# The scan's maxima rows through memory and a GpSimd mask, and the next unit's scores ahead of this unit's updates

## The chip, the cores and the metric

The kernel is one launch on one core of a Trainium2 chip. The metric is device time in microseconds (us), the median over runs; one further execution was profiled.

## The reference

The reference is a two-layer diffusion backbone. Each layer runs four token mixers side by side on 1024 latent tokens and 256 context tokens, projects their outputs, and then applies a feed-forward part (dense in layer 0, top-2 of 8 experts in layer 1). The change concerns the two recurrent mixers, gated linear attention (GLA) and mLSTM, each run forwards and backwards:

```python
def gla_scan(...):      # per chunk
    scores = jnp.where(mask, q_dec @ (k * exp(-cum)).T, 0.0)
    o = scores @ v + q_dec @ s_prev
    s = decay * s + upd
def mlstm_scan(...):    # per chunk
    d_log = jnp.where(mask, cum[..., :, None] - cum[..., None, :] + ig[..., None, :], -jnp.inf)
    m_row = jnp.maximum(inter_log, jnp.max(d_log, axis=-1))
    s = jnp.exp(d_log - m_row[..., None]) * (q @ k.T)
    num = s @ v + w_int * (q @ c_prev)
    out = num / jnp.maximum(jnp.abs(den), jnp.exp(-m_row))
```

## The kernel before, in words

The kernel is a chain of phases. Each phase is a block in which every engine has its own program; the orders are written out by hand and the engines meet at counting semaphores. All engines meet at the end of each block, and GpSimd then clears the phase's semaphores.

Per layer, `phase_side` (L613) computes the gates, the decays, the chunked gating and the Fourier mixing. Its VectorE part fills `mx`, the running maxima of the mLSTM gates: rows 0 to 3 are the four heads forwards, rows 32 to 35 backwards, each 1280 long (L896 to L899). The semaphore `stk` counts three later VectorE steps (L914 to L916).

`phase_scan` (L940) walks U = 20 units per layer, 40 in all: ten tiles of 128 tokens in each of two directions, even units forwards, odd ones backwards. A unit `u` has on each engine:

- TensorE: three transposes into the PSUM banks KT and TR (L987, L989); the maxima rows, spread over all partitions and masked with a large number, into the bank MB (one product of the identity with the mask, L994, then four of a selector with `mx`, L997); the mLSTM scores into SM (L1004); the GLA scores into SG (L1011), which wait for the states of the unit before (`v_st`); the products with the states into OG and OC (L1016, L1018); the GLA output (L1021), after VectorE has masked the scores (`v_sg`); the mLSTM output (L1026); the state updates, GLA's into the upper half of OG (L1031), mLSTM's into SG (L1034).
- ScalarE: a copy of a transpose (L1045), then four exponentials of the maxima rows into `ex` (L1048).
- GpSimd: the queries, masked by head, `qg` (L1066) and `qm` (twice L1068). It may run ahead until the scores of the unit two before are done.
- VectorE: the weighted keys `kw` (L1087), masked copy of the GLA scores `sg` (L1090), the mLSTM weights (L1094), the GLA output added or copied (L1098 or L1100), the mLSTM numerator (`tmp` L1103, `num` L1105), denominator and output (L1108 to L1117), and the state updates `dsg` (L1121), `dsm` (L1123), `Sm` (L1125), `Sg` (L1126), `Sm` again (L1128) and `Sp` (L1130), which ends the unit (`v_st`).

In the first ten units each tile is met for the first time and its output is written; in the last ten it is added to (L1098; L1114 with L1115 in place of L1117). The phase after, `phase_mix_project`, forms the mixers' output and projects it.

Of the kernel before, what the change touches and what calls it, by code (L numbers as in the profile page):

```python
# [18 lines left out]
ACT = mybir.ActivationFunctionType  # L19
# [3 lines left out]
P = 128  # L23
D = 1024
# [588 lines left out]
def phase_side(nc, io, S, l, FM, TM, M, ctx_out):  # L613
# [8 lines left out]
    with Phase(nc, f"side{l}") as ph:  # L622
# [23 lines left out]
        folded, ymm, yev, dused, cdone, zout = (ph.sem(n) for n in (  # L646
            "folded", "y_done", "y_ready", "dft_used", "ctx_z_done", "z_ready"))
# [14 lines left out]
        with nc.Block() as block:  # L662

            @block.sync
            def _(sp):
# [19 lines left out]
                for j in range(NPIECE + (1 if ctx_out else 0)):  # L685
                    piece(j)

# [252 lines left out]
def phase_scan(nc, io, S, l, FM, TM, M):  # L940

    U = 2 * NT
    with Phase(nc, f"scan{l}") as ph:
# [12 lines left out]
        pe_tr, pe_mb, pe_sg, pe_sm, pe_og, pe_om, pe_u = (ph.sem(n) for n in (  # L956
            "transposed", "max_rows_done", "gla_scores_done", "mlstm_scores_done", "gla_out_done", "mlstm_out_done", "updates_done"))
        a_kdt, a_ex = ph.sem("kdt_ready"), ph.sem("ex_ready")
        g_q = ph.sem("masked_q_ready")
# [7 lines left out]
        mx, tg, dcol, qd, kd, em, vx, og, om = (M[k] for k in ("mx", "tg", "dcol", "qd", "kd", "em", "vx", "og", "om"))  # L967
        TR, SG, OG, KT, MB, SM, OI, OC = range(8)
        mq, mk = (2, 3), (4, 5)
        sel8 = c("sel8").rearrange("p (a t) -> p a t", t=P)  # L970
# [6 lines left out]
        with nc.Block() as block:  # L977

            @block.tensor
            def _(pe):  # L980
                for u in range(U):
                    d, n, t = unit(u)

                    if u >= 1:
                        pe.wait_ge(a_kdt, u)
                        pe.wait_ge(v_kw, u)
                    nc.tensor.transpose(ps[:, KT, 0:P], kd[:, d, t], c("ident"))  # L987
                    for j in range(2):
                        x = nc.tensor.transpose(ps[:, TR, (j + 1) * P:(j + 2) * P], FM[:, mk[j], t], c("ident"))  # L989
                    x.then_inc(pe_tr, 1)  # L990

                    if u >= 1:
                        pe.wait_ge(a_ex, u)
                    nc.tensor.matmul(ps[:, MB, :].rearrange("p (h t) -> p h t", t=P), c("ident"),  # L994
                                     c("negF" if d == 0 else "negB").unsqueeze(1).to_broadcast([P, NH, P]), start=True, stop=False, skip_group_check=True)
                    for h in range(NH):
                        x = nc.tensor.matmul(ps[:, MB, h * P:(h + 1) * P], sel8[32 * d:32 * d + 4, 4 * d + h, :], mx[32 * d:32 * d + 4, t],  # L997
                                             start=False, stop=(h == NH - 1), skip_group_check=True)
                    x.then_inc(pe_mb, 1)
# [6 lines left out]
                    x.then_inc(pe_sm, 1)  # L1006
                    if u >= 1:
                        pe.wait_ge(v_st, u)
                    else:
                        pe.wait_ge(v_init, 1)  # L1010
                    nc.tensor.matmul(ps[:, SG, :], kd[:, d, t], qg[:, d, :, :].rearrange("p a b -> p (a b)"),  # L1011
                                     start=True, stop=True).then_inc(pe_sg, 1)
                    if u >= 1:
                        pe.wait_ge(v_og, u)
                        pe.wait_ge(v_om, u)
                    nc.tensor.matmul(ps[:, OG, 0:256], qd[:, d, t], Sp[:, d, :], start=True, stop=False, skip_group_check=True)  # L1016
# [6 lines left out]
                    x.then_inc(pe_og, 1)  # L1023
                    pe.wait_ge(v_w, u + 1)
                    for h in range(NH):
                        x = nc.tensor.matmul(ps[:, OI, h * 65:(h + 1) * 65], ex[:, d, h, :], vx[:, n, h, :], start=True, stop=True)  # L1026
                    x.then_inc(pe_om, 1)

                    pe.wait_ge(a_kdt, u + 1)
                    pe.wait_ge(v_og, u + 1)  # L1030
                    nc.tensor.matmul(ps[:, OG, 256:512], kdt[:, d, :], TM[:, n, 0:256], start=True, stop=True)  # L1031
                    pe.wait_ge(v_kw, u + 1)
                    for j in range(2):
                        x = nc.tensor.matmul(ps[:, SG, j * 130:(j + 1) * 130], kw[:, d, 2 * j:2 * j + 2, :].rearrange("p a b -> p (a b)"),  # L1034
# [1501 lines left out]
```

## Time and profile before

| | us |
|---|---|
| median of 3 runs | 5304.72 |
| lowest, highest | 5299.55, 5308.38 |
| the profiled execution, its own time | 5301.93 |
| its span | 5300.3 |

| engine | busy us | share of the span |
|---|---|---|
| TensorE (PE) | 4911.6 | 93% |
| VectorE (DVE) | 2886.4 | 54% |
| ScalarE (ACT) | 2189.5 | 41% |
| GpSimd (POOL) | 296.0 | 6% |

In the page, PE is the matmul side of TensorE and PEld its weight loads. PEclk is the share of TensorE's full clock that was granted; 1.00 is 2.4 GHz, 0.50 is 1.2 GHz. A matmul of a float32 operand shows as two records, so four matmuls are x8. A row of the timeline can merge several records of one line; its second number is the time from the first record's start to the last one's end, and a square bracket gives how long the engine sat idle before it and what ended that. A row of busy time by stretch gives the stretch, its length, the busy time and count of instructions of PE, PEld, DVE, ACT and POOL in turn, then PEclk, the DMA share and GB/s. Most of the span is the expert phase at the end; the two scans stand at 434 to 613 us and at 2205 to 2383 us.

### The profile page before, as it was taken

How to read it: one execution, taken by the hardware profiler on the slowest of the kernel's cores; microseconds unless marked ns; L12 is line 12 of the kernel's file. 1: busy time of each engine (PE TensorE's matmuls, PEld its weight loads, DVE VectorE, ACT ScalarE, POOL GpSimd, SP SyncE). 2: the span in 40 equal slices, each digit the busy share in tenths (PEclk: the TensorE clock that was granted, in tenths of full speed). 3: DMA queues.
4: the chain of work that ended last, by engine and by line, in shares of the span. 5: the costliest groups of instructions: out<-in, count | busy, mean ns of one | idle time of the engine just before them, and what ended most of it. 6: DMA issues, size and time to landing. Idle time of an engine off the chain costs nothing. (4 is left out here: it accounts for less than half of the span.)

```text
span 5300.3 us, 62249 instructions
## 1 busy us (share of the span) xinstructions
PE 4911.6 (93%) x23448; PEld 4002.3 (76%) x23449; DVE 2886.4 (54%) x2935; ACT 2189.5 (41%) x2253; POOL 296.0 (6%) x303
## 2 busy tenths in 40 slices
PE   6998896999999899897799999999999999999994
PEld 5876665888888678576688888888888888888883
DVE  4367643111133356674764549984696454558476
ACT  3242322111132233313654438773675343446364
POOL 1002210000000010122000000000000000000001
PEclk8998997999999899898899999999999999999996
DMA  5320354222255442104775559995797555569576
GB/s 201 111 85 8 114 189 129 99 96 88 75 191 184 147 141 88 35 1 150 311 286 180 202 192 361 379 354 192 272 378 276 188 200 190 191 231 342 185 285 247
DMA packets 253712, 1003.56 MB, mean 189 GB/s; under 512 B 31840, under 2 KB 96672, under 8 KB 169248
## 3 DMA queue, kind: packets, MB, share of 16 engines
q1 hardware_dynamic: 239152, 945.70, 49.2%
q0 software_dynamic: 10992, 40.90, 2.1%
q10 hardware_dynamic: 3456, 15.47, 0.7%
q8 instruction: 71, 1.16, 0.1%
q14 instruction: 41, 0.34, 0.0%
HBM read 948.77 MB, written 53.22 MB: 189 GB/s over the span
## 5 line engine op out<-in xcount | busy, mean ns | idle before, releaser
L1997 PE MATMUL ps<-moe_gate_up_hi,moe_xh 128*128 128x512 f32 x2464 | 961.8, 390 | 4.4 <-DVE moe_gate_up_lo L2173 4.4
L2173 DVE TENSOR_TENSOR moe_gate_up_lo<-moe_wst,moe_gate_up_hi 128x2048 fp32r<-128x2048 f32 x424 | 952.4, 2285 | 16.6 <-ACT moe_gate_up_hi L2080 16.6
L1997 PE MATMUL ps<-moe_gate_up_hi,moe_xl 128*128 128x512 f32 x2464 | 960.9, 390 | 0.0
L1997 PE MATMUL ps<-moe_gate_up_lo,moe_xh 128*128 128x512 f32 x2464 | 958.9, 389 | 0.0
L2080 ACT CAST moe_gate_up_hi<-moe_wst 128x2048 fp32r<-128x2048 f32 x424 | 791.0, 1920 | 9.7 <-issue 7.0
L2276 DVE TENSOR_TENSOR moe_down_lo<-moe_wst,moe_down_hi 128x2048 fp32r<-128x2048 f32 x210 | 480.2, 2290 | 158.9 <-ACT moe_down_hi L2118 158.2
L2282 DVE TENSOR_TENSOR norm<-moe_sil,ps 128x512 f32<-128x512 f32 x210 | 143.6, 684 | 743.5 <-ACT moe_sil L2124 743.5
L1997 PEld LDWEIGHTS ps<-moe_gate_up_hi,moe_xh 128*128 128x128 f32 x2464 | 462.8, 188 | 101.3 <-DVE moe_gate_up_lo L2173 6.3
L1997 PEld LDWEIGHTS ps<-moe_gate_up_hi,moe_xl 128*128 128x128 f32 x2464 | 462.7, 188 | 96.2
L1997 PEld LDWEIGHTS ps<-moe_gate_up_lo,moe_xh 128*128 128x128 f32 x2464 | 462.8, 188 | 95.4
L2124 ACT ACTIVATE moe_sil<-ps 128x512 f32<-128x512 f32 x210 | 125.9, 600 | 984.2 <-PE ps L1997 984.0
L2118 ACT CAST moe_down_hi<-moe_wst 128x2048 fp32r<-128x2048 f32 x210 | 403.6, 1922 | 72.8 <-PE ps L2017 72.7
L1596 PE MATMUL ps<-hh,up_wh 128*128 128x512 f32 (+1 forms) x1056 | 377.0, 357 | 49.7 <-DVE up_wl L1653 49.7
L2017 PE MATMUL ps<-moe_down_hi,moe_ah 128*128 128x512 f32 x1232 | 399.9, 405 | 9.6 <-DVE moe_al L2287 9.6
L2017 PE MATMUL ps<-moe_down_lo,moe_ah 128*128 128x512 f32 x1232 | 383.3, 392 | 0.0
L2017 PE MATMUL ps<-moe_down_hi,moe_al 128*128 128x512 f32 x1232 | 380.3, 390 | 0.0
L1596 PE MATMUL ps<-hl,up_wh 128*128 128x512 f32 (+1 forms) x1056 | 374.9, 355 | 0.0
L1596 PE MATMUL ps<-hh,up_wl 128*128 128x512 f32 (+1 forms) x1056 | 374.6, 355 | 0.0
L1664 DVE TENSOR_TENSOR up_a<-up_sil,ps 128x512 f32<-128x512 f32 (+1 forms) x66 | 39.6, 600 | 482.0 <-PE ps L1596 481.0
L577 DVE TENSOR_TENSOR proj_w_lo<-proj_w_raw,proj_w_hi 128x1024 fp32r<-128x1024 f32 x122 | 151.6, 1243 | 233.6 <-ACT proj_w_hi L489 232.6
L489 ACT CAST proj_w_hi<-proj_w_raw 128x1024 fp32r<-128x1024 f32 x122 | 127.8, 1047 | 353.8 <-PE ps L433 194.0
L2017 PEld LDWEIGHTS ps<-moe_down_hi,moe_al 128*128 128x128 f32 x1232 | 231.2, 188 | 52.4
(385 smaller groups left out, 7600.1 us busy)
## 6 DMA issues: line engine op xcount, KB each, us to landing
moe_wst<-in_moe_packed SPq DMA_DIRECT2D x634, 1024.0 KB, 6.8
proj_w_raw<-in_w_in_packed SPq DMA_DIRECT2D x122, 512.0 KB, 3.4
down_wst<-in_ffn_w_down SPq DMA_DIRECT2D x66, 512.0 KB, 3.6
up_ada_w<-in_ada_packed SPq DMA_DIRECT2D x12, 2048.0 KB, 8.3
ys_d<-moe_y POOLq DMA_DIRECT2D x15, 1024.0 KB, 4.5
tail_ada_w<-in_ada_packed SPq DMA_DIRECT2D x7, 2048.0 KB, 9.8
a_d<-up_a ACTq DMA_DIRECT2D x22, 640.0 KB, 3.0
FM<-in_w_out_packed SPq DMA_DIRECT2D x27, 512.0 KB, 3.9
```

The source lines that it names most:

```text
L489: nc.scalar.copy(wh[:, p % 2, :], raw[:, p % RAW, :]).then_inc(w_hi, 1)
L577: nc.vector.tensor_tensor(wlo[:, p % 2, :], raw[:, p % RAW, :], wh[:, p % 2, :].bitcast(F32), ALU.subtract).then_inc(split, 1)
L1596: x = nc.tensor.matmul(ps[:, 2 * g + kind, :n], w[:, s, kind, k, :], h[:, k, t0:t0 + n], start=(k == 0 and j == 0), stop=(k == KD - 1 and ...
L1664: nc.vector.tensor_tensor(a[:, s, t0:t0 + n], sil[:, g, :n], ps[:, 2 * g + 1, :n], ALU.mult).then_inc(used, 1)
L1997: x = nc.tensor.matmul(ps[:, 2 * (q % 2) + i, :], xx[:, k, t], w[:, q % 2, k, :], start=(k == 0 and j == 0), stop=(k == KD - 1 and j == 2))
L2017: x = nc.tensor.matmul(ps[:, Y0 + 2 * i + half, :], aa[:, q % 2, i, c, :], w[:, q % 2, c, half * 512:(half + 1) * 512], start=(q == 0 and ...
L2080: nc.scalar.copy(guh[:, q % 2, 4 * j:4 * j + 4, :], wst[:, slot(n), :].rearrange("p (k n) -> p k n", k=4)).then_inc(hi, 1)
L2118: nc.scalar.copy(dnh[:, q % 2, :, :], wst[:, slot(n), :].rearrange("p (k n) -> p k n", k=2)).then_inc(hi, 1)
L2124: nc.scalar.activation(sil[:, :, :], ps[:, 2 * (q % 2):2 * (q % 2) + 2, 0:W], ACT.Silu).then_inc(silu, 1)
L2173: nc.vector.tensor_tensor(gul[:, q % 2, k, :], wst[:, slot(n), :].rearrange("p (k n) -> p k n", k=4), guh[:, q % 2, k, :].bitcast(F32), AL ...
L2276: nc.vector.tensor_tensor(dnl[:, q % 2, :, :], wst[:, slot(n), :].rearrange("p (k n) -> p k n", k=2), dnh[:, q % 2, :, :].bitcast(F32), AL ...
L2282: nc.vector.tensor_tensor(a[:, q % 2, :, :, :].rearrange("p i c f -> p i (c f)"), sil[:, :, :], ps[:, 2 * (q % 2):2 * (q % 2) + 2, W:2 * W ...
```

## The change

- In `phase_side`, SyncE waits for `stk` and stores the eight used rows of `mx` to a new tensor `mx_d` in memory, then waits for both stores.
- In `phase_scan`, SyncE loads for each unit the four rows of its direction and tile, repeated to all 128 partitions, into a ring of four tiles `mxr`. From the fifth unit on it waits for the exponentials of the unit four before.
- GpSimd, after the masked queries of a unit, adds the mask to the loaded tile in place. ScalarE's exponentials read that tile and wait for GpSimd in place of TensorE. The products L994 and L997 are gone.
- TensorE's order is new. For unit `u`: products with the states; GLA output; transposes of `u+1`; mLSTM output of `u`; mLSTM scores and GLA scores of `u+1`; state updates of `u`. The GLA scores wait for VectorE's masked copy of the unit before and no longer for its states.
- The updates of the GLA state go to the upper half of KT, those of mLSTM to the bank that held the maxima, now UM.

```diff
...
+                sp.wait_ge(stk, 1)
+                for d in range(2):
+                    sp.dma_start(S["mx_d"][4 * d:4 * d + 4, :], mx[32 * d:32 * d + 4, :]).then_inc(mxs, 16)
+                sp.wait_ge(mxs, 32)
...
-        g_q = ph.sem("masked_q_ready")
+        g_q, g_mx = ph.sem("masked_q_ready"), ph.sem("max_rows_masked")
+        RING = 4
+        mxr = ph.sb("max_rows", [P, RING, NH, P])
+        mld = [ph.sem(f"max_rows_loaded{s}") for s in range(RING)]
...
-        mx, tg, dcol, qd, kd, em, vx, og, om = (M[k] for k in ("mx", "tg", "dcol", "qd", "kd", "em", "vx", "og", "om"))
-        TR, SG, OG, KT, MB, SM, OI, OC = range(8)
+        tg, dcol, qd, kd, em, vx, og, om = (M[k] for k in ("tg", "dcol", "qd", "kd", "em", "vx", "og", "om"))
+        TR, SG, OG, KT, UM, SM, OI, OC = range(8)
         mq, mk = (2, 3), (4, 5)
-        sel8 = c("sel8").rearrange("p (a t) -> p a t", t=P)
...
-                for u in range(U):
+
+                def turn(u):
                     d, n, t = unit(u)
-
                     if u >= 1:
                         pe.wait_ge(a_kdt, u)
                         pe.wait_ge(v_kw, u)
+                    if u >= 2:
+                        pe.wait_ge(v_st, u - 1)
                     nc.tensor.transpose(ps[:, KT, 0:P], kd[:, d, t], c("ident"))
                     for j in range(2):
-                        x = nc.tensor.transpose(ps[:, TR, (j + 1) * P:(j + 2) * P], FM[:, mk[j], t], c("ident"))
+                        x = nc.tensor.transpose(ps[:, TR, j * P:(j + 1) * P], FM[:, mk[j], t], c("ident"))
                     x.then_inc(pe_tr, 1)
 
-                    if u >= 1:
-                        pe.wait_ge(a_ex, u)
-                    nc.tensor.matmul(ps[:, MB, :].rearrange("p (h t) -> p h t", t=P), c("ident"),
-                                     c("negF" if d == 0 else "negB").unsqueeze(1).to_broadcast([P, NH, P]), start=True, stop=False, skip_group_check=True)
-                    for h in range(NH):
-                        x = nc.tensor.matmul(ps[:, MB, h * P:(h + 1) * P], sel8[32 * d:32 * d + 4, 4 * d + h, :], mx[32 * d:32 * d + 4, t],
-                                             start=False, stop=(h == NH - 1), skip_group_check=True)
-                    x.then_inc(pe_mb, 1)
+                def mlstm_scores(u):
+                    d, n, t = unit(u)
                     if u >= 1:
                         pe.wait_ge(v_w, u)
                     pe.wait_ge(g_q, u + 1)
@@ -1004,15 +1006,27 @@
                         x = nc.tensor.matmul(ps[:, SM, j * 256:(j + 1) * 256], FM[:, mk[j], t],
...
                     x.then_inc(pe_sm, 1)
+
+                def gla_scores(u):
+                    d, n, t = unit(u)
                     if u >= 1:
-                        pe.wait_ge(v_st, u)
-                    else:
-                        pe.wait_ge(v_init, 1)
+                        pe.wait_ge(v_sg, u)
+                    pe.wait_ge(g_q, u + 1)
                     nc.tensor.matmul(ps[:, SG, :], kd[:, d, t], qg[:, d, :, :].rearrange("p a b -> p (a b)"),
                                      start=True, stop=True).then_inc(pe_sg, 1)
+
+                turn(0)
+                mlstm_scores(0)
+                gla_scores(0)
+                for u in range(U):
+                    d, n, t = unit(u)
+                    following = u + 1 < U
+                    pe.wait_ge(v_init, 1)
                     if u >= 1:
                         pe.wait_ge(v_og, u)
                         pe.wait_ge(v_om, u)
+                    if u >= 2:
+                        pe.wait_ge(v_st, u - 1)
                     nc.tensor.matmul(ps[:, OG, 0:256], qd[:, d, t], Sp[:, d, :], start=True, stop=False, skip_group_check=True)
                     for j in range(2):
                         nc.tensor.matmul(ps[:, OC, j * 130:(j + 1) * 130], FM[:, mq[j], t], Sm[:, d, j, :], start=True, stop=True)
...
                     x.then_inc(pe_og, 1)
+                    if following:
+                        turn(u + 1)
                     pe.wait_ge(v_w, u + 1)
                     for h in range(NH):
                         x = nc.tensor.matmul(ps[:, OI, h * 65:(h + 1) * 65], ex[:, d, h, :], vx[:, n, h, :], start=True, stop=True)
                     x.then_inc(pe_om, 1)
-
-                    pe.wait_ge(a_kdt, u + 1)
-                    pe.wait_ge(v_og, u + 1)
-                    nc.tensor.matmul(ps[:, OG, 256:512], kdt[:, d, :], TM[:, n, 0:256], start=True, stop=True)
+                    if following:
+                        mlstm_scores(u + 1)
+                        gla_scores(u + 1)
+
+                    if u >= 1:
+                        pe.wait_ge(v_st, u)
+                    pe.wait_ge(a_kdt, u + 2 if following else u + 1)
+                    nc.tensor.matmul(ps[:, KT, 256:512], kdt[:, d, :], TM[:, n, 0:256], start=True, stop=True)
                     pe.wait_ge(v_kw, u + 1)
                     for j in range(2):
-                        x = nc.tensor.matmul(ps[:, SG, j * 130:(j + 1) * 130], kw[:, d, 2 * j:2 * j + 2, :].rearrange("p a b -> p (a b)"),
+                        x = nc.tensor.matmul(ps[:, UM, j * 130:(j + 1) * 130], kw[:, d, 2 * j:2 * j + 2, :].rearrange("p a b -> p (a b)"),
                                              vx[:, n, 2 * j:2 * j + 2, :].rearrange("p a b -> p (a b)"), start=True, stop=True)
                     x.then_inc(pe_u, 1)
...
                         act.wait_ge(pe_u, u - 1)
                     act.wait_ge(pe_tr, u + 1)
                     nc.scalar.copy(kdt[:, d, :], ps[:, KT, 0:P]).then_inc(a_kdt, 1)
-                    act.wait_ge(pe_mb, u + 1)
+                    act.wait_ge(g_mx, u + 1)
                     for h in range(NH):
-                        x = nc.scalar.activation(ex[:, d, h, :], ps[:, MB, h * P:(h + 1) * P], ACT.Exp,
+                        x = nc.scalar.activation(ex[:, d, h, :], mxr[:, u % RING, h, :], ACT.Exp,
                                                  bias=tg[:, n, 0, d, h:h + 1], scale=-1.0)
                     x.then_inc(a_ex, 1)
 
-            if l == 1:
-                @block.sync
-                def _(sp):
+            @block.sync
+            def _(sp):
+                if l == 1:
                     with nc.allow_non_contiguous_dma(reason="a column set as a vector"):
                         sp.dma_start(cols(S["g2_d"]), S["mod"][:, 1, 40:48, 0]).then_inc(filled, 16)
+                for u in range(U):
+                    d, n, t = unit(u)
+                    if u >= RING:
+                        sp.wait_ge(a_ex, u - RING + 1)
+                    sp.dma_start(mxr[:, u % RING, :, :], S["mx_d"][4 * d:4 * d + 4, t].unsqueeze(0).to_broadcast([P, NH, P])).then_inc(mld[u % RING], 16)
+                if l == 1:
                     sp.wait_ge(filled, 16)
 
...
                         x = nc.gpsimd.tensor_tensor(qm[:, d, 2 * j:2 * j + 2, :], FM[:, mq[j], t].unsqueeze(1).to_broadcast([P, 2, P]),
                                                     bc(c("row2"), P), ALU.mult)
                     x.then_inc(g_q, 1)
+                    pool.wait_ge(mld[u % RING], 16 * (u // RING + 1))
+                    nc.gpsimd.tensor_tensor(mxr[:, u % RING, :, :], mxr[:, u % RING, :, :],
+                                            c("negF" if d == 0 else "negB").unsqueeze(1).to_broadcast([P, NH, P]), ALU.add).then_inc(g_mx, 1)
...
                     dve.wait_ge(pe_tr, u + 1)
-                    nc.vector.tensor_tensor(kw[:, d, :, :], ps[:, TR, P:3 * P].rearrange("p (h c) -> p h c", c=HD),
+                    nc.vector.tensor_tensor(kw[:, d, :, :], ps[:, TR, 0:2 * P].rearrange("p (h c) -> p h c", c=HD),
...
                     dve.wait_ge(pe_u, u + 1)
-                    nc.vector.scalar_tensor_tensor(out=dsg[:, :], in0=ps[:, OG, 256:512], scalar=em[:, d, 2, n:n + 1], in1=c("blockg"),
+                    nc.vector.scalar_tensor_tensor(out=dsg[:, :], in0=ps[:, KT, 256:512], scalar=em[:, d, 2, n:n + 1], in1=c("blockg"),
                                                    op0=ALU.mult, op1=ALU.mult)
-                    nc.vector.tensor_tensor(dsm[:, :, :], ps[:, SG, 0:260].rearrange("p (a b) -> p a b", b=130),
+                    nc.vector.tensor_tensor(dsm[:, :, :], ps[:, UM, 0:260].rearrange("p (a b) -> p a b", b=130),
                                             c("blockm").unsqueeze(1).to_broadcast([P, 2, 130]), ALU.mult)
...
-         (("xT_d", (P, KD, T)), ("xs_d", (SEQ, D)), ("ys_d", (NUNIT * UNIT, D)), ("g2_d", (D,)), ("a_d", (P, DFF // P, T)))}
+         (("xT_d", (P, KD, T)), ("xs_d", (SEQ, D)), ("mx_d", (2 * NH, T)), ("ys_d", (NUNIT * UNIT, D)), ("g2_d", (D,)), ("a_d", (P, DFF // P, T)))}
...
```

## Rows read from the trace of the kernel before

**Rows 1.** Busy time by stretch in layer 0's scan.

```profile
434.80:444.80 10.00, 9.67 (x27) 6.30 (x25) 3.79 (x7) 1.41 (x5) 6.03 (x9) 0.50 0.00 1
445.00:612.00 167.00, 158.58 (x913) 119.39 (x912) 124.72 (x324) 26.77 (x95) 37.41 (x52) 1.00 0.00 1
```

**Rows 2.** Timeline of one early unit: start, length, engine, line, what, idle before.

```profile
527.83 0.73 DVE L1090 COPY_PREDICATED scan_sg<-cst,ps 128x512 f32<-128x512 int32 x1 [0.76 <-PE ps L1011]
527.94 1.04 POOL L1066 TENSOR_TENSOR scan_qg<-qd,cst 128x512 f32<-128x512 f32 x1 [6.13 <-PE ps L1011]
...
528.62 1.10 PE L1021 MATMUL ps<-TM,scan_sg 128*128 128x64 f32 x8
...
528.94 1.19 POOL L1068 TENSOR_TENSOR scan_qm<-FM,cst 128x256 f32<-128x256 f32 x2
...
529.56 1.06 PE L1026 MATMUL ps<-vx,scan_ex 128*128 128x65 f32 x8
...
530.45 0.65 PE L1031 MATMUL ps<-TM,scan_kdt 128*128 128x256 f32 x2
530.65 0.43 DVE L1103 TENSOR_TENSOR scan_tmp<-ps,tg 128x260 f32<-128x260 f32 x1 [0.47 <-PE ps L1026]
...
530.94 0.61 PE L1034 MATMUL ps<-vx,scan_kw 128*128 128x130 f32 x4
...
531.39 0.27 PE L987 MATMUL ps<-cst,kd 128*128 128x128 f32 x1
...
531.71 1.02 PE L994 MATMUL ps<-cst 128*128 128x512 f32 x2
...
532.53 0.48 DVE L1121 SCALAR_TENSOR_TENSOR scan_dsg<-ps,em,cst 128x256 f32<-128x256 f32 x1
...
533.26 0.42 DVE L1125 TENSOR_TENSOR scan_Sm<-scan_Sm,dcol 128x260 f32<-128x260 f32 x1
...
534.96 0.42 DVE L1087 TENSOR_TENSOR scan_kw<-ps,tg 128x256 f32<-128x256 f32 x1
534.98 0.30 PEld L1011 LDWEIGHTS ps<-scan_qg,kd 128*128 128x128 f32 x2 [0.50 <-DVE scan_Sp L1130]
534.98 1.12 PE L1011 MATMUL ps<-scan_qg,kd 128*128 128x512 f32 x2
...
535.94 0.59 PE L1016 MATMUL ps<-scan_Sp,qd 128*128 128x256 f32 x2
...
536.14 0.73 DVE L1090 COPY_PREDICATED scan_sg<-cst,ps 128x512 f32<-128x512 int32 x1 [0.76 <-PE ps L1011]
```

**Rows 3.** The same view of a late unit, in which outputs are added to.

```profile
591.10 0.43 DVE L1103 TENSOR_TENSOR scan_tmp<-ps,tg 128x260 f32<-128x260 f32 x1 [0.47 <-PE ps L1026]
...
593.43 0.48 DVE L1121 SCALAR_TENSOR_TENSOR scan_dsg<-ps,em,cst 128x256 f32<-128x256 f32 x1
```

**Rows 4.** Timeline of GpSimd and VectorE in layer 0's projection phase.

```profile
651.12 4.60 POOL L1259 TENSOR_TENSOR TM<-TM,tail_ng 128x2048 f32<-128x2048 f32 x1 [2.95 <-ACT TM L1353]
...
653.00 2.76 DVE L1421 TENSOR_SCALAR tail_ms<-tail_ms 128x32 f32<-128x32 f32 x1
```

**Rows 5.** Timeline of TensorE: first matmuls after idle holes at full clock.

```profile
124.65 0.47 PE L435 MATMUL ps<-proj_h_hi,proj_w_hi 128*128 128x512 f32 x1 [2.36 <-DVE proj_h_lo L534]
...
242.38 0.47 PE L435 MATMUL ps<-proj_h_hi,proj_w_hi 128*128 128x512 f32 x1 [2.35 <-DVE proj_h_lo L534]
...
649.39 0.48 PE L1298 MATMUL ps<-tail_mix_hi,tail_w_parts 128*128 128x256 f32 x2 [3.63 <-DVE tail_w_parts L1408]
```

**Rows 6.** Busy time by stretch, right after the first two holes of Rows 5.

```profile
124.70:128.00 3.30, 3.30 (x15) 2.74 (x16) 3.30 (x5) 3.30 (x6) 0.00 (x0) 1.00 0.07 26
243.60:246.80 3.20, 3.20 (x9) 2.46 (x8) 3.20 (x5) 3.20 (x6) 0.00 (x0) 0.50 0.50 169
```

**Rows 7.** Timeline of TensorE: GLA scores of layer 0's first unit.

```profile
441.03 1.92 PE L1011 MATMUL ps<-scan_qg,kd 128*128 128x512 f32 x2
```

**Rows 8.** DMA issues by line: size of one, median us from issue to landing.

```profile
tail_ng<-in_gla_norm_g SPq DMA_DIRECT2D x2, 128.0 KB, 4.9
```

More of the change, by code:

```diff
@@ L645, in phase_side @@
             "vectors_loaded", "sgu_loaded", "vectors_zeroed", "stacks_zeroed", "dve_step", "act_step"))
-        folded, ymm, yev, dused, cdone, zout = (ph.sem(n) for n in (
-            "folded", "y_done", "y_ready", "dft_used", "ctx_z_done", "z_ready"))
+        folded, ymm, yev, dused, cdone, zout, mxs = (ph.sem(n) for n in (
+            "folded", "y_done", "y_ready", "dft_used", "ctx_z_done", "z_ready", "maxima_stored"))
         zmm, zmin, zabs, zln, lmin, lln = (ph.sem(n) for n in ("gate_done", "gate_min", "gate_abs", "gate_log", "forget_min", "forget_log"))
@@ L955, in phase_scan @@
         Sm = ph.sb("Sm", [P, 2, 2, 130])
-        pe_tr, pe_mb, pe_sg, pe_sm, pe_og, pe_om, pe_u = (ph.sem(n) for n in (
-            "transposed", "max_rows_done", "gla_scores_done", "mlstm_scores_done", "gla_out_done", "mlstm_out_done", "updates_done"))
+        pe_tr, pe_sg, pe_sm, pe_og, pe_om, pe_u = (ph.sem(n) for n in (
+            "transposed", "gla_scores_done", "mlstm_scores_done", "gla_out_done", "mlstm_out_done", "updates_done"))
         a_kdt, a_ex = ph.sem("kdt_ready"), ph.sem("ex_ready")
-        g_q = ph.sem("masked_q_ready")
+        g_q, g_mx = ph.sem("masked_q_ready"), ph.sem("max_rows_masked")
+        RING = 4
+        mxr = ph.sb("max_rows", [P, RING, NH, P])
+        mld = [ph.sem(f"max_rows_loaded{s}") for s in range(RING)]
         qg = ph.sb("qg", [P, 2, NH, P])
```

## Prediction

> **What bounds the kernel now.** I read the page first, for the scans' place in the span, then the busy time by stretch, then the timeline of single units. TensorE looks saturated in the scan: busy 158.58 of 167.00 us at a granted clock of 1.00 [rows 1]. The reader is not to stop there. In the timeline the GLA scores (L1011) stand idle for 0.50 us and are released by VectorE's `Sp` (L1130), and the masked copy (L1090) stands idle for 0.76 us until those scores land [rows 2]. So the loop is one chain over both engines: masked copy, GLA output, mLSTM output, VectorE from `tmp` (L1103) to `Sp`, GLA scores, masked copy. From one masked copy to the next it takes 536.14 - 527.83 = 8.31 us in an early unit [rows 2]. A late unit spends 593.43 - 591.10 = 2.33 us from `tmp` to `dsg` (L1121) where the early one spends 532.53 - 530.65 = 1.88 [rows 2, 3], so it takes 8.31 + 0.45 = 8.76 us. The mean is 8.54. The maxima products L994 and L997 lie beside VectorE's chain. They bound nothing, but they keep TensorE active. I count 38 such periods, 19 per layer; the first unit of a layer runs at half clock before and presumably after.
>
> **The new order, at full clock and with free engines.** I set the start of a masked copy to 0 and add TensorE's queue up in its new order, all from rows 2.
> - To the first matmul of the GLA output: 528.62 - 527.83 = 0.79.
> - GLA output: 529.56 - 528.62 = 0.94.
> - Transposes of the next unit, moved ahead of the mLSTM output: 531.71 - 531.39 = 0.32. Their waits (keys, copy, states of the unit before) are long met.
> - mLSTM output: 530.45 - 529.56 = 0.89.
> - mLSTM scores and GLA scores of the next unit, now ahead of the updates. Each streams 1024 columns as L994 does. L994 shows 1.02, of which 0.16 is a tail that the next matmul overlaps (L1034 shows 0.61 and is followed after 531.39 - 530.94 = 0.45). That makes 0.86 each, 1.72 for both.
> - Updates: L1031 0.49 (530.94 - 530.45), L1034 0.61, and 0.03 until VectorE sees it (`tmp` at 530.65 after L1026's end at 530.62).
>
> The sum is 0.79 + 0.94 + 0.32 + 0.89 + 1.72 + 0.49 + 0.64 = 5.79 us. VectorE starts `tmp` at 0.79 + 0.94 + 0.32 + 1.06 + 0.03 = 3.14 and wants the updates at 3.14 + 1.88 = 5.02, or 5.47 in a late unit. So it waits there 0.77 or 0.32 us where it waited for nothing: the wait for the GLA scores has become one for the updates queued behind them. From `dsg` to `kw` are 534.96 - 532.53 = 2.43, and `kw` takes 0.42 [rows 2]; then the masked copy starts without a wait. The period is 5.79 + 2.43 + 0.42 = 8.64 for both kinds of unit, against 8.54. The reordering alone gives 0.10 x 38 = 4 us back to the slow side.
>
> **What it does to GpSimd and VectorE.** GpSimd's work of a unit starts when a unit's GLA scores land, 527.94 - 527.83 = 0.11 after the masked copy could start [rows 2]. Before, that lies beside the masked copy and the outputs. Now these scores land at 0.79 + 0.94 + 0.32 + 0.89 + 0.86 + 1.12 = 4.92, so GpSimd starts at about 5.07. It has 1.04 + 1.19 us and the added mask, of the form of L1066, 1.04: 3.27 us, until 8.3. VectorE's `Sm` (L1125) wants to start at 5.79 + 533.26 - 532.53 = 6.52 and has four instructions with all operands in SBUF until the end of the unit. What such a meeting costs is seen elsewhere [rows 4]: a VectorE instruction of 32 columns began at 653.00 and lasted 2.76 us, until 655.76, and GpSimd's instruction ended at 651.12 + 4.60 = 655.72. In rows 2 the masked copy reads PSUM and shows 0.73 us beside GpSimd. So VectorE's updates can be held by what GpSimd still has to do, between 0 and 8.3 - 6.5 = 1.8 us per unit. I take 1.4, nearer to the upper end, since rows 4 show whole instructions held and the four alternate with GpSimd's. A gain is excluded: nothing there becomes shorter.
>
> The Trainium skill, page "SBUF — State Buffer", section "Who interferes with whom", says that a VectorE instruction with two SBUF inputs and a GpSimd instruction that reads SBUF exclude each other, and that one with a single SBUF input is free. By that rule the term lies between the same 0 and 1.8. [...]
>
> **What it does to TensorE's clock.** Per unit TensorE now has 0.94 + 0.32 + 0.89 + 1.72 + 0.49 + 0.45 of the above, and the products with the states, 0.59 - 0.16 = 0.43 and, with L1034's size, 0.45: 5.69 us. They wait for nothing and stand ahead of the next masked copy. The rest is one hole, 8.64 - 5.69 - 0.16 = 2.79 us as the records show it, and 2.79 + 1.4 = 4.2 with GpSimd's term. At full clock the trace has eight idle holes of 2.35 to 2.94 us, two of which stand here [rows 5]. After the one at 242.38 the clock stood at 0.50, after the one at 124.65 at 1.00 [rows 6]; in all, five of the eight were followed by 0.50. It has four of 3.63 us and more at full clock (one in rows 5), and all four lowered it. So with the hole at 4.2 us I expect the clock to fall in every unit. At 0.50 streaming takes twice as long: the GLA scores 1.92 instead of 1.12 [rows 2, 7]. The low stretch of rows 6 lasts at least 3.2 us, and one at the start of the scan lasts through 10.00 us in which TensorE is 97% busy with small products [rows 1]. The middle case: low over the GLA output, transposes, mLSTM output, mLSTM scores and half of the GLA scores, which is all on the path: 0.94 + 0.32 + 0.89 + 0.86 + 0.43 = 3.4 us more. Bounds: 1.6 (3.2 us at half speed) and 5.0 (the whole path of 5.79 - 0.79).
>
> **Smaller parts.** The loads run three units ahead, over 24 us, against 4.9 us to landing for another repeated row [rows 8]; hidden, and if they were not, 4.9 x 38 would be at stake. Behind GpSimd's wait for a load stand the next unit's `qg` and `qm`, and TensorE's scores behind these, but they are prepared two units ahead. The first load has no such lead: at worst 2 us per layer. SyncE's stores of `mx` start while TensorE's transposes and VectorE's gating of that block are still to come, which hides them; if nothing did, 4.9 us per layer. SyncE has nothing else queued behind them. ScalarE's exponentials only change their source. I count these at 0 to 10 us in all, and take 0.
>
> **The sum.** 8.64 + 1.4 + 3.4 = 13.44 us per unit, 4.90 more than 8.54; times 38 is 186 us. The profiled execution took 5301.93 us, so 5488. It lies 2.8 us below the median of the runs, so that a median would come out at 5491; the forecast stays at 5488, since the difference is far below the bounds. The removed 2 us of maxima products per unit come off TensorE, and nothing of them off the time.
>
> **Rivals.**
> - Clock alone. GpSimd holds nothing up, and the hole is 2.79 us; five to eight in eight units fall: (0.10 + 2.2 to 3.4) x 38 = 87 to 133, about 5410. For: the masked queries never met these instructions before, so rows 4 are from another phase. Against: their length.
> - GpSimd alone, the clock holds: 1.5 x 38 = 57, about 5359. Against: four of four long holes.
> - Low all the time: 8.64 + 1.8 + 5.0 = 15.4, 6.9 x 38 = 262, about 5564. For: rows 1, ten us at 0.50. Against: the scores and updates stream densely enough to look like the stretch after 243.60, which returned to full clock.
> - Neither: 4 us, about 5306. The Trainium skill, page "TensorE: Matmul & The Clock Gate", section "Why this matters for your kernels", warns of idle gaps only from a length that lies above the 2.79 us; by that rule this is the result of a free GpSimd. Rows 5 and 6, with a fall after 2.35 us, speak against it.
> - The other side, faster: VectorE's own work is the bound. It decides at the wait for the updates. If they land before 5.02, 0.77 us sooner than I count, the period is 5.02 + 2.43 + 0.42 = 7.87, late 8.32, in the mean 0.44 below before: -17 us, 5285. It needs the clock to hold as well.
> - That the change doesn't do what it says is covered by these: the maxima products go, but the time does not hang on them.
>
> **How the numbers follow.** Chances: both effects 0.55, clock alone 0.20, low all the time 0.09, GpSimd alone 0.04, neither 0.05, faster 0.07. The likeliest has its own range, 0.9 + 2.6 to 1.8 + 4.2 per unit: 5440 to 5537. With the clock-alone case and part of the heaviest the range is 5380 to 5545, and about 2 in 10 lie outside. A measurement of this kernel can tell some 0.2% (11 us) from no change: faster 0.07, same 0.05, slower 0.88.
>
> **What would show it.** Right, if the profile of after shows: `dsg` idle before it and released by L1034; TensorE idle 4 us once per unit, before L1021; PEclk well below 1.00 in the scans; `Sm` longer than its 0.42 us [rows 2], or `Sg` and `Sp` longer than before, with GpSimd's three lines beside them. Wrong, if PEclk stays at 1.00 or the VectorE lengths are unchanged, or if idle time stands before the exponentials, released by GpSimd or a load.

## The result, and the profile after

| | before | after |
|---|---|---|
| median of 4 runs each, us | 5303.45 | 5453.23 |
| lowest, highest | 5299.55, 5308.38 | 5447.0, 5453.51 |
| the profiled execution, its own time | 5301.93 | 5453.49 |
| its span | 5300.3 | 5451.8 |
| scan of layer 0, first transpose to last `Sp` | 179.1 | 246.2 |
| scan of layer 1 | 178.1 | 257.8 |
| mean of the 19 periods, layer 0 and 1 | 8.57, 8.53 | 12.04, 12.69 |
| time at granted clock 0.50 in the scans | 11.9, 8.0 | 113.0, 131.5 |

The kernel became slower by 150 us, ratio 1.0279 (95% interval 1.0264 to 1.0293). The forecast was 186 us. The two scans hold 67.1 + 79.7 = 146.8 of the 151.5 us by which the span grew. So the scans are the place to read.

Busy time by stretch of the kernel after, in the stretch of [rows 1] and in one that holds layer 1's scan:

```profile
445.00:612.00 167.00, 116.66 (x523) 97.59 (x521) 100.43 (x222) 20.14 (x70) 53.51 (x58) 0.78 0.08 23
2190.00:2430.00 240.00, 164.32 (x647) 122.75 (x645) 141.51 (x276) 53.73 (x105) 53.59 (x62) 0.79 0.12 37
```

In the same 167 us TensorE is now busy for 116.66 where it was for 158.58, and the clock granted to it is 0.78 where it was 1.00. It issues 523 matmuls where it issued 913: the maxima products are gone, and fewer units fit in. The waits of the kernel after from 450 to 630 us (engine, what it was about to write, line, releaser; us in total, times, longest):

```profile
PE ps L1035 <- DVE scan_sg L1119: 58.2, 15, 4.0
DVE scan_dsg L1150 <- PE ps L1054: 27.6, 15, 2.8
DVE scan_tmp L1132 <- PE ps L1042: 24.4, 14, 1.8
```

L1035 is the GLA output (L1021 before), L1119 the masked copy (L1090), L1054 the mLSTM update (L1034), L1132 is `tmp` (L1103). TensorE's 58.2 us over 15 units are one hole of 3.9 us per unit. VectorE waits 1.8 us per unit for the updates and 1.7 for the mLSTM output. Neither wait stood in [rows 2] at such a length. The timeline of the kernel after shows two units that follow on each other, at full clock and at half clock:

```profile
522.26 1.91 PE L1015 MATMUL ps<-scan_qg,kd 128*128 128x512 f32 x2
...
524.32 1.04 POOL L1092 TENSOR_TENSOR scan_qg<-qd,cst 128x512 f32<-128x512 f32 x1 [9.03 <-PE ps L1015]
...
525.28 0.49 DVE L1150 SCALAR_TENSOR_TENSOR scan_dsg<-ps,em,cst 128x256 f32<-128x256 f32 x1 [2.64 <-PE ps L1054]
525.32 1.19 POOL L1094 TENSOR_TENSOR scan_qm<-FM,cst 128x256 f32<-128x256 f32 x2
...
526.02 0.77 DVE L1154 TENSOR_TENSOR scan_Sm<-scan_Sm,dcol 128x260 f32<-128x260 f32 x1
526.46 1.45 POOL L1098 TENSOR_TENSOR scan_max_rows<-scan_max_rows,cst 128x512 f32<-128x512 f32 x1
526.82 1.36 DVE L1155 SCALAR_TENSOR_TENSOR scan_Sg<-scan_Sg,em,scan_dsg 128x256 f32<-128x256 f32 x1
528.22 0.43 DVE L1157 TENSOR_TENSOR scan_Sm<-scan_Sm,scan_dsm 128x260 f32<-128x260 f32 x1
...
530.06 1.10 PE L1035 MATMUL ps<-TM,scan_sg 128*128 128x64 f32 x8 [3.93 <-DVE scan_sg L1119]
...
534.75 1.02 PE L1015 MATMUL ps<-scan_qg,kd 128*128 128x512 f32 x2
...
538.28 1.44 POOL L1098 TENSOR_TENSOR scan_max_rows<-scan_max_rows,cst 128x512 f32<-128x512 f32 x1
538.63 1.37 DVE L1157 TENSOR_TENSOR scan_Sm<-scan_Sm,scan_dsm 128x260 f32<-128x260 f32 x1
...
541.41 1.91 PE L1035 MATMUL ps<-TM,scan_sg 128*128 128x64 f32 x8 [3.88 <-DVE scan_sg L1119]
```

The same GLA output takes 1.10 us in one unit and 1.91 in the next, the same GLA scores 1.91 and 1.02: both levels of the clock, on one form each. `Sg` (L1155) takes 1.36 us, and it ends 0.27 us after GpSimd's mask does (526.46 + 1.45 = 527.91, 528.18). In the unit behind it the same happens to the second `Sm`, L1157: 1.37 us. The kernel before, in the unit of [rows 2], has these two and `Sp` at

```profile
533.71 0.48 DVE L1126 SCALAR_TENSOR_TENSOR scan_Sg<-scan_Sg,em,scan_dsg 128x256 f32<-128x256 f32 x1
534.23 0.43 DVE L1128 TENSOR_TENSOR scan_Sm<-scan_Sm,scan_dsm 128x260 f32<-128x260 f32 x1
534.58 0.35 DVE L1130 TENSOR_SCALAR scan_Sp<-scan_Sg,em 128x256 f32<-128x256 f32 x1
```

Nearly all periods of the kernel after are either 11.4 or about 13.0 us, in turns or with two long ones in a row.

### The profile page after: what moved, and what is told of

It is laid out like the page before. It is cut to its first block and busy times, and to the rows that moved or that the text cites. A ratio compares the mean times of both kernels' runs of the same rounds, so it can differ in the third digit from the quotient of the medians.

```text
span 5451.8 us, 61617 instructions
## 1 busy us (share of the span) xinstructions
PE 4917.8 (90%) x23048; PEld 4033.4 (74%) x23049; DVE 2927.3 (54%) x2935; ACT 2191.4 (40%) x2253; POOL 358.2 (7%) x343
## 5 line engine op out<-in xcount | busy, mean ns | idle before, releaser
L2109 ACT CAST moe_gate_up_hi<-moe_wst 128x2048 fp32r<-128x2048 f32 x424 | 791.5, 1921 | 10.1 <-issue 8.1
```

What stands on the lines that cost most here:

```text
L2109: nc.scalar.copy(guh[:, q % 2, 4 * j:4 * j + 4, :], wst[:, slot(n), :].rearrange("p (k n) -> p k n", k=4)).then_inc(hi, 1)
```

## The experiments

"Period" is the time from one masked copy to the next; medians come with their lowest and highest, and ratios are to the kernel before on the same chip, with 95% intervals. The cuts of code are shortened: a line that begins with `...` tells in words what stands there. The kernel before ran at 5305.29 beside the first four kernels and at 5305.0 beside the last four.

**One half alone: the memory path under the old order.** TensorE's queue is as before (transposes, scores, outputs, updates of one unit), with its old waits and banks, but the maxima come from memory and GpSimd masks them.

```
- turn(0); mlstm_scores(0); gla_scores(0)
  for u in range(U):
-     ... GLA output of u, turn(u + 1), mLSTM output of u, scores of u + 1, updates of u
+     ... turn(u), scores of u, outputs of u, updates of u
```

> The old order of TensorE's work, with the maxima through memory and GpSimd's mask. Theory (the clock falls after holes, GpSimd holds VectorE's updates): the chain over VectorE is the old one of 8.31 and 8.76 us, and GpSimd's 3.5 us end before the updates begin, so their lengths stay at 0.42 to 0.49 us. But without the maxima products TensorE has a hole of about 2.2 us before the GLA scores in each unit, the size at which the clock fell in five of eight cases before. I expect it to fall in about half of the units, at 1 to 2.7 us each: 20 to 100 us over the kernel before, 50 in the middle. Rival 1 (the whole loss comes with the new order; the clock only shows it): within 10 us of before. Rival 2 (the maxima products bounded something after all): faster.

Measured: 5359.19 us (5358.67 to 5362.74), ratio 1.0105 (1.0088 to 1.0122): +54 us without any new order. Timeline of this kernel, one unit:

```profile
524.76 0.35 DVE L1137 TENSOR_SCALAR scan_Sp<-scan_Sg,em 128x256 f32<-128x256 f32 x1
525.16 1.77 PE L1009 MATMUL ps<-scan_qg,kd 128*128 128x512 f32 x2 [2.24 <-DVE scan_Sp L1137]
526.96 0.73 DVE L1097 COPY_PREDICATED scan_sg<-cst,ps 128x512 f32<-128x512 int32 x1 [1.40 <-PE ps L1009]
```

Where the maxima products L994 and L997 stood, TensorE is now idle: 2.24 us where [rows 2] has 0.50. The scores behind the hole take 1.77 us instead of 1.12. `Sm`, `Sg` and `Sp` have their old lengths (0.42, 0.49, 0.43, 0.35), so GpSimd holds nothing here. The time at half clock is 72.2 and 74.9 us, where before had 11.9 and 8.0. The removed products had kept the clock up; taking them away costs by itself. Not all of the 54 us are the clock's: layer 1's first period is 17.3 us here and 8.3 in the kernel before, and those 9 us come from a late row (below).

**Fill the hole.** The kernel after, with four products per unit that nothing reads, before TensorE's wait for the masked copy.

```
+ for _ in range(4):
+     nc.tensor.matmul(ps[:, OI, :], c("ident"), FM[:, mk[0], 0:512], start=True, stop=True)
  pe.wait_ge(v_sg, u + 1)
```

> The changed kernel with four further products of 128x512 in each unit, issued in TensorE's hole before the wait for the masked GLA scores, 0.86 us each at full clock; their result is never read. Theory: the hole of about 4 us is filled, the clock stays at 1.00 in the scans, and the period falls from 12.3 to 8.64 + 1.2 (GpSimd's share) = 9.8 us: 5350 to 5375 us in all, some 85 less than the changed kernel, although TensorE has 137 us more to do. Rival (the low clock is a bystander, the chain of waits makes the time): no gain, 5453 us or more.

Measured: 5367.07 (5360.04 to 5370.27), ratio 1.0114 (1.0097 to 1.0131). More work on TensorE, and 86 us less than the kernel after. The time at half clock falls to 10.8 and 16.5 us, the periods to 9.7 (early) and 10.1 (late). In its timeline VectorE is still held beside GpSimd, in an early unit and in a late one:

```profile
525.21 0.72 DVE L1157 SCALAR_TENSOR_TENSOR scan_Sg<-scan_Sg,em,scan_dsg 128x256 f32<-128x256 f32 x1
525.61 1.44 POOL L1100 TENSOR_TENSOR scan_max_rows<-scan_max_rows,cst 128x512 f32<-128x512 f32 x1
525.96 1.38 DVE L1159 TENSOR_TENSOR scan_Sm<-scan_Sm,scan_dsm 128x260 f32<-128x260 f32 x1
...
528.75 1.11 PE L1037 MATMUL ps<-TM,scan_sg 128*128 128x64 f32 x8 [0.45 <-DVE scan_sg L1121]
...
592.01 1.04 POOL L1094 TENSOR_TENSOR scan_qg<-qd,cst 128x512 f32<-128x512 f32 x1 [6.36 <-PE ps L1015]
...
592.11 1.22 DVE L1146 TENSOR_TENSOR TM<-TM,scan_tmp 128x256 f32<-128x256 f32 x1
```

L1146 is the sum of a late unit's output, which the prediction did not count among the held ones. It shows 0.42 us where it meets nothing and 1.21 to 1.22 in 14 of the 20 late units.

**Move GpSimd out of VectorE's way.** The kernel after, with GpSimd's work of a unit held until VectorE has updated the states of the unit three before, so that it lies beside the masked copy as before.

```
  pool.wait_ge(pe_sg, u - 1)
+ pool.wait_ge(v_st, max(u - 2, 1))
```

> The changed kernel, but GpSimd starts a unit's work when VectorE has finished the states of the unit three before, that is beside keys, masked copy and weights, and not when GLA scores land. Theory: VectorE's Sm, Sg and Sm again go from means of 0.49, 0.87 and 1.15 us back to 0.42, 0.49 and 0.43, 1.2 us per unit; TensorE's hole shrinks from 4 to about 2.8 us, so that the clock falls in fewer units or as often. 46 us less by the lengths alone, 5360 to 5410 us. Rival (those lengths come from something else than GpSimd): lengths and time unchanged, 5453 us.

Measured: 5375.61 (5369.91 to 5379.04), ratio 1.0133 (1.0116 to 1.015): 78 us less than the kernel after. `Sm`, `Sg`, `Sm`, `Sp` are back to 0.42, 0.48, 0.43 and 0.35 us. The hole shrinks from 3.9 to 2.71 us, the clock still falls (72.8 and 83.1 us at half), and the period is 10.2 us in nearly every unit:

```profile
522.76 1.10 PE L1035 MATMUL ps<-TM,scan_sg 128*128 128x64 f32 x8 [2.71 <-DVE scan_sg L1120]
...
529.42 0.48 DVE L1151 SCALAR_TENSOR_TENSOR scan_dsg<-ps,em,cst 128x256 f32<-128x256 f32 x1 [2.37 <-PE ps L1054]
```

This is the rival "clock alone" made real: it gives +70 us, with the late row of layer 1 in it, where the prediction put 87 to 133.

**Both.** The early GpSimd, and three fillers. This leaves the new order and the late row of layer 1.

```
+ for _ in range(3):
+     nc.tensor.matmul(ps[:, OI, :], c("ident"), FM[:, mk[0], 0:512], start=True, stop=True)
  pe.wait_ge(v_sg, u + 1)
  ...
+ pool.wait_ge(v_st, max(u - 2, 1))
```

> Both of the above, with three further products per unit for the smaller hole. Theory: nothing but the new order is left, at 8.64 us per unit against 8.54: 4 us, and the late first load of layer 1, 5 to 10 us: 5305 to 5325 us. Rival (a third cause beside clock and GpSimd): above 5340 us.

Measured: 5317.55 (5313.59 to 5320.47), ratio 1.0025 (1.0015 to 1.0034). Timeline and busy time of this kernel:

```profile
527.20 0.48 DVE L1153 SCALAR_TENSOR_TENSOR scan_dsg<-ps,em,cst 128x256 f32<-128x256 f32 x1 [0.70 <-PE ps L1056]
```
```profile
445.00:580.00 135.00, 132.79 (x687) 94.42 (x686) 99.62 (x257) 23.12 (x80) 54.65 (x64) 1.00 0.10 30
```

The period is 8.5 us for both kinds of unit, and VectorE waits 0.70 us for the updates that are queued behind the next unit's scores: the prediction's "new order, at full clock and with free engines" as worked out (8.64, and 0.77 us idle). Taking both costs out wins 136 of the 150 us back. What is left over the kernel before, 12 us, is in the first periods: 17.8 us in layer 1 and 11.7 in layer 0, where the kernel before has 8.3 and 9.1. A part of that comes from the fillers themselves, which the first unit runs at half clock: without them (the kernel before this one) the two are 16.2 and 9.2.

The two costs do not simply add. GpSimd's place alone costs 49.5 us (5367.07 - 5317.55), the clock alone 58.1 (5375.61 - 5317.55), both together 135.7. The other 28 us come from the meeting of the two: VectorE held longer makes TensorE's hole 3.9 instead of 2.71 us, and half of the units then have the long low stretch that the third kernel (early GpSimd alone) does not show.

**The first period of layer 1.** It is long in every kernel with the memory path so far (18.6, 17.3, 18.6, 16.2, 17.8 us). GpSimd and ScalarE in the kernel after:

```profile
2292.42 1.26 POOL L1098 TENSOR_TENSOR scan_max_rows<-scan_max_rows,cst 128x512 f32<-128x512 f32 x1 [8.17 <-DMA scan_max_rows<-mx_d]
...
2293.72 1.28 ACT L1068 ACTIVATE scan_ex<-scan_max_rows,tg 128x128 f32<-128x128 f32 x4 [13.22 <-POOL scan_max_rows L1098]
```

The mask waits 8.17 us for the first row from memory, and the exponentials 13.22 for the mask. The row landed 13.4 us after its issue, against a median of 3.3 over the 40 loads. It was issued at 2279.71 behind the store of a column set as a vector (L1076, `g2_d`), which only layer 1 has on the same queue.

**Another place for the score products.** If the cost is a hole that the clock sees and updates queued behind scores, then the updates should go first. TensorE issues the outputs of a unit, its updates, and then the next unit's scores; GpSimd stays early. The products with the states now wait for the states of the unit before (`v_st`), and GLA's update goes back to the upper half of OG.

```
- ... GLA output of u, turn(u + 1), mLSTM output of u, scores of u + 1, updates of u
+ ... GLA output of u, mLSTM output of u, updates of u, turn(u + 1), scores of u + 1
+ nc.tensor.matmul(ps[:, OG, 256:512], kdt[:, d, :], TM[:, n, 0:256], start=True, stop=True)
+ pool.wait_ge(v_st, max(u - 2, 1))
```

> GpSimd early as in e3, and another order on TensorE: GLA output, mLSTM output, state updates of this unit, and only then transposes and scores of the next (GLA's update goes back to the upper half of OG, read before the next products with the states). No further products. Theory: VectorE finds the updates landed at 0.79 + 0.94 + 0.89 + 0.49 + 0.64 = 3.75 us, wants them at 2.82 + 1.88 = 4.70, so it no longer waits: period 4.70 + 2.43 + 0.42 = 7.55 us, late 8.00. TensorE's idle time of 2 us stands in two holes of some 1.2 and 0.5 us, and the clock stays at 1.00. 29 us less than before by the periods, some 10 more for the late first load of layer 1: 5280 to 5295 us. Rival (the clock falls with any idle time of this amount): 5340 us or more.

Measured: 5302.91 (5299.29 to 5307.99), ratio 0.9997 (0.9988 to 1.0007), outside the expectation. The periods are 7.5 and 7.9 us where the clock holds, below the 8.31 and 8.76 of before, as reckoned; but it holds in only some. Where two holes of 1.2 and 0.5 us were expected, there is one in front of the products with the states (L1030), and beside periods of 7.5 stand others of 9.0 to 9.8. The time at half clock is 52.8 and 63.0 us. Timeline, two units, and the busy time of one stretch:

```profile
513.62 0.67 PE L1030 MATMUL ps<-scan_Sp,qd 128*128 128x256 f32 x2 [1.47 <-DVE scan_Sp L1157]
...
522.77 0.59 PE L1030 MATMUL ps<-scan_Sp,qd 128*128 128x256 f32 x2
```
```profile
517.00:524.00 7.00, 7.00 (x26) 5.51 (x26) 5.48 (x15) 1.44 (x5) 0.97 (x2) 0.61 0.11 33
```

After the hole of 1.47 us that ends at 513.62 the next unit ran partly at half speed (the last line above: PEclk 0.61 from 517 to 524 us); it took so long that TensorE had no hole left at 522.77.

**The store later.** The same, with the store of the column issued after the first four loads.

```
- if l == 1:
+ if l == 1 and u == RING:
      sp.dma_start(cols(S["g2_d"]), ...)
```

> As e5, but in layer 1 SyncE issues the small column store of the gates (1024 single elements) after the first four loads of maxima rows, not before them. Theory (the first load waits behind that store): GpSimd's first mask in layer 1 no longer idles 8 us, the first period falls from about 17 to 12 us or less, and the time is 4 to 8 us below e5. Rival (the first load is slow by itself, as the first read of a tensor just written): the same as e5.

Measured: 5291.54 (5285.7 to 5296.23), ratio 0.9976 (0.9967 to 0.9986). Layer 1's first period is 7.8 us instead of 15.4, and the whole takes 11 us less than with the store in its old place, more than the 4 to 8 expected; the first period gives 7.6 of them. The column store was the cause of the late row. The clock still falls, mostly in the late units, whose hole is longer. Timeline, an early and two late units (the clock stayed at 1.00 after the first two of these holes and fell to 0.50 at 556.1 us, after the third):

```profile
531.23 0.67 PE L1030 MATMUL ps<-scan_Sp,qd 128*128 128x256 f32 x2 [1.47 <-DVE scan_Sp L1157]
...
546.62 0.67 PE L1030 MATMUL ps<-scan_Sp,qd 128*128 128x256 f32 x2 [1.93 <-DVE scan_Sp L1157]
...
554.54 0.67 PE L1030 MATMUL ps<-scan_Sp,qd 128*128 128x256 f32 x2 [1.93 <-DVE scan_Sp L1157]
```

**One filler in that hole.** The same, with one unread product ahead of the wait for `Sp` of the products with the states.

```
+ nc.tensor.matmul(ps[:, OI, :], c("ident"), FM[:, mk[0], 0:512], start=True, stop=True)
  if u >= 1:
      pe.wait_ge(v_st, u)
```

> As e6, with one further product of 128x512 per unit in the hole ahead of the products with the states. Theory: where the clock held in e6 it only fills idle time, the time is that of e6 within 5 us; if it fell in e6 in some units, it is lower here.

Measured: 5281.99 (5277.34 to 5286.38), ratio 0.9961 (0.9947 to 0.9975): 0.4% faster than the kernel before. The scans take 164.0 and 164.5 us. Timeline and busy time:

```profile
528.45 0.70 PE L1031 MATMUL ps<-scan_Sp,qd 128*128 128x256 f32 x2 [0.52 <-DVE scan_Sp L1158]
```
```profile
445.00:580.00 135.00, 121.77 (x695) 93.51 (x695) 109.42 (x286) 24.51 (x86) 61.43 (x72) 1.00 0.11 30
```

All periods past the first two are 7.5 or 7.9 us, and only some 10 us per scan are at half clock, in the first unit. One product of 0.95 us or so (1.47 - 0.52), with no use to the result, gains 9.5 us over the kernel without it, between medians whose runs just overlap (5277.34 to 5286.38 against 5285.7 to 5296.23).

**The same order with GpSimd late.** The kernel with the late store, without GpSimd's added wait.

```
- pool.wait_ge(v_st, max(u - 2, 1))
```

> As e6, but GpSimd starts when the GLA scores land, as in the changed kernel. They now land at about 5.9 us, so GpSimd's 3.5 us run from 6.0 on beside Sm's second instruction and Sp, and on beside keys and masked copy. Theory: the second Sm and Sp are lengthened by up to one GpSimd instruction each, 0.6 to 1.2 us per unit, 20 to 45 us above e6, more if the larger hole lowers the clock. Rival (only the order matters, as no wait is added): the same as e6.

Measured: 5340.17 (5338.2 to 5341.23), ratio 1.007 (1.0053 to 1.0087): 49 us above the kernel with the early GpSimd, a little more than expected. GpSimd's place depends on when the scores land; in the units in which it meets VectorE's updates, `Sg` takes up to 1.36 us and `Sp` up to 1.21. Timeline, one such unit:

```profile
573.65 1.54 POOL L1091 TENSOR_TENSOR scan_qm<-FM,cst 128x256 f32<-128x256 f32 x2
574.00 0.72 DVE L1154 TENSOR_TENSOR scan_Sm<-scan_Sm,scan_dsm 128x260 f32<-128x260 f32 x1
574.65 0.70 DVE L1156 TENSOR_SCALAR scan_Sp<-scan_Sg,em 128x256 f32<-128x256 f32 x1
```

The periods are mostly 9.0 to 10.7, and 89.0 and 86.3 us of the scans are at half clock (44.4 and 52.1 with GpSimd early). GpSimd's delays seem to be paid a second time, as longer holes: TensorE's idle time before L1030 is up to 3.2 us, and the time at half clock is nearly twice that of the kernel with GpSimd early.

## Why the prediction was right, and where it was off

Direction, both mechanisms and the range were right; 5453 lies 35 us under the 5488. That it is 35 and not more is luck in part: terms that were counted 47 us too high met 12 us that were put at nothing.

- **The chain before** (8.31, 8.76, mean 8.54, 38 periods): the 38 periods of the trace have a mean of 8.55.
- **The new order, 8.64.** With both costs removed it ran at 8.5. The wait moved to the updates as described, 0.70 us measured, 0.77 forecast. The term was +0.10 and is about 0.
- **GpSimd holds VectorE, 1.4.** The kernel after has, from 434 to 660 us (line, engine, operation, shapes, count; busy us, mean ns):

```profile
L1157 DVE TENSOR_TENSOR scan_Sm<-scan_Sm,scan_dsm 128x260 f32<-128x260 f32 x17 | 19.5, 1149 | 0.6
L1155 DVE SCALAR_TENSOR_TENSOR scan_Sg<-scan_Sg,em,scan_dsg 128x256 f32<-128x256 f32 x17 | 14.8, 870 | 0.6
L1154 DVE TENSOR_TENSOR scan_Sm<-scan_Sm,dcol 128x260 f32<-128x260 f32 x17 | 8.3, 488 | 0.0
L1098 POOL TENSOR_TENSOR scan_max_rows<-scan_max_rows,cst 128x512 f32<-128x512 f32 x20 | 28.3, 1413 | 0.0
```

  Against 0.43, 0.48 and 0.42 that is 0.72 + 0.39 + 0.07 = 1.18 us per unit. The kernel with four fillers shows the same at full clock: 9.70 - 8.53 = 1.17 in an early unit; its late unit pays 10.13 - 8.53 = 1.60, since there the output's sum is held too and stands in no wait. The rest of the gap to 1.4: `Sp` was counted as one of the held ones, and its row shows 0.342. The mask was estimated at 1.04 from L1066 and takes 1.26 alone and 1.41 here.
- **The clock, 3.4.** This is the term that was mis-sized. The mean period of the 38 is 12.37 us; without layer 1's first (18.6) it is 12.20. Take off 8.5 and 1.18, and 2.5 us are left for the clock, inside the bounds of 1.6 and 5.0. It is a remainder, and holds what the two costs make together. Busy time by stretch of the kernel after, two units in a row:

```profile
524.50:531.20 6.70, 2.77 (x22) 2.49 (x21) 5.18 (x10) 0.00 (x0) 3.41 (x4) 1.00 0.01 1
531.30:534.60 3.30, 3.30 (x14) 3.03 (x13) 1.54 (x6) 1.44 (x5) 0.00 (x0) 0.50 0.07 20
534.80:541.40 6.60, 2.73 (x15) 1.95 (x13) 5.01 (x10) 0.00 (x0) 3.80 (x4) 1.00 0.09 26
541.60:548.30 6.70, 6.70 (x25) 5.82 (x26) 2.53 (x8) 1.44 (x5) 0.00 (x0) 0.50 0.14 39
```

  After each hole TensorE works without a pause, first at 0.50 and then at 1.00. A low stretch of which it is busy throughout costs half of its length: 6.70 gives 3.35, the forecast's 3.4, and 3.30 gives 1.65, its lower bound. The two periods come out of it: 8.53 + 1.18 + 1.65 = 11.36 and 8.53 + 1.18 + 3.35 = 13.06, measured 11.4 and about 13.0. Short and long stretches are about equally many, which makes 2.5. So the step that failed is the middle case "low over the GLA output, transposes, mLSTM output, mLSTM scores and half of the GLA scores" for every unit: the clock did fall in every unit with such a hole, but only in about every second for so long. In the third kernel (early GpSimd) nearly each unit has one short stretch, and 8.5 + 1.65 is its period of 10.2. (3.4 - 2.5) x 38 = 34 us, with the order's (8.64 - 8.5) x 38 = 5 and GpSimd's (1.4 - 1.18) x 38 = 8, is 47 us too much.
- **Slips in the working.** The trace of before has thirteen holes of 3.6 us and more that begin at full clock, not four; all thirteen were followed by 0.50, so the conclusion stands. "Streaming takes twice as long" is shown there with 1.92 and 1.12, which is 1.7 times; the pair of the kernel after, 1.91 and 1.02, is nearer. The upper end of the likeliest case is 5302 + 38 x 6.1 = 5534, not 5537. And the held instruction of [rows 4] has one SBUF tensor as input, which does not go with "one with a single SBUF input is free" (see the last section).
- **"First load at worst 2 us per layer", taken as 0.** It was 6 to 9 us, in layer 1 only: 18.6 against 12.2 in the kernel after, 17.8 against 8.5 with both costs removed, 15.4 against 7.8 with the store moved, which is the clean pair. The step overlooked what stands ahead of the load on SyncE's queue. The other loads are hidden as predicted: the exponentials wait only for the mask, and hardly then (5.0 us in 76 instructions).
- **Between the scans** the kernel after takes 1597.8 us where before took 1591.6, one profiled execution each. The other kernels with the memory path show 1593.8 to 1600.1. No experiment was made on it; it stays open, with about 6 us. These 6 and the 6 of the first period offset part of the 47: 186 - 47 + 12 = 151, where the profiled executions differ by 151.56; so close a sum owes something to rounding.
- **The rivals.** "Low all the time" was wrong: the clock came back to 1.00 in nearly every unit (not in the last one of a scan). "Neither" and "faster" needed a hole that leaves the clock alone; the filler kernels show what that would have given, 5317.55 for this order. The Trainium skill, page "TensorE: Matmul & The Clock Gate", section "Why this matters for your kernels", was cited as warning of idle gaps only from a length above 2.79 us. The runs speak against it as a limit: holes of 2.71 us (third kernel), 2.24 (first) and some of 1.47 (fifth) were followed by 0.50.
- **The signs to look for** all stood there: `dsg` idle and released by the updates, TensorE idle 3.9 us ahead of the GLA output, PEclk at 0.78, `Sm` and `Sg` long beside GpSimd's rows. `Sp`, named with them, kept its length.

## What to carry to other kernels

Before taking work off an engine whose clock can fall, ask what that work was covering: here products that bounded nothing kept TensorE's hole at 0.50 us, and without them the same order lost 54 us, some 45 of them apart from the late row of layer 1. When GpSimd is given more to do, set the place of that work by a wait of its own, beside VectorE's instructions that read PSUM; one line was worth 78 us. And when the next unit's work is issued ahead, put it behind whatever the other engine wants next: with GpSimd early in both and no filler, updates first gave 5302.91 us and scores first 5375.61.

## What the runs showed of the hardware

- The length of a hole alone does not decide the clock. In the kernel with the late store, holes of 1.47 us in a row (494 to 539 us) left it at 1.00 and those of 1.93 were mostly followed by 0.50; in the kernel with the store in its old place holes of the same 1.47 (for one that which ends at 513.62) were followed by 0.50 as well. After 3.9 us it fell each time, after 2.71 in nearly every unit of the third kernel (not after the one that ends at 614.7 us). With 0.45 to 0.98 us, in the kernels with four fillers and with one, it fell in no unit past the first three periods. Which of two equal holes lowers it was not settled.
- GpSimd's sum of 128 x 512 in place took 1.26 us alone and up to 1.45 beside VectorE, against 1.04 for `qg` of the same shape, whose operands are broadcast. Both sides of a meeting get longer.
- `dsg` and `dsm`, which read PSUM, met GpSimd's instructions in 34 of the 40 units of the kernel after and kept 0.48 and 0.42 us; the masked copy kept its 0.73 beside `qg` in the kernel before. Of those in SBUF alone the first `Sm` (L1154), whose second operand is a broadcast column, met them in 34 units and was longer in 10; the mean above is 488 ns. In the kernel with four fillers the output's sum (L1146), two tensors in SBUF, took 1.22 instead of 0.42. `Sp` has a single SBUF tensor as input and was not tested in the kernel after, since it starts when the mask is over; in the last experiment it was held in all 20 units in which it met GpSimd, for 0.70 to 1.21 us. The prediction took the rule of the Trainium skill as "one with a single SBUF input is free". In that form its own [rows 4] speak against it: the held instruction there is itself a TENSOR_SCALAR with one tensor as input. The Trainium skill, page "SBUF — State Buffer", section "Who interferes with whom", makes the exception: it lists `tensor_scalar` among those that can enter a mode with both ports and so can contend. The runs agree with that half: `Sp` takes 0.35 us by itself.
- A store of 1024 single elements made the load behind it on the queue land after 13.4 us instead of 3.3. With the store moved behind four loads, layer 1's first period fell from 15.4 to 7.8 us.
